# Trading two steps of SyncE's queue at the end of a rotated tile

## The reference

```
h = rmsnorm(x, norm_g[i]);  proj = h @ w_in[i]
A: forgetting attention, 8 heads x 64        (qa, ka, va, fa, za)        no rotary
B: sparse attention, 8 query heads, 2 groups (qb, kcb, vcb, ksb, vsb, kwb, vwb, gb, zb)
   qb, ksb, kwb go through rope(); compressed, selected and window branches, gated
C: differential attention, 4 heads x 2 maps  (qc, kc, vc, zc)            qc, kc go through rope()
merged = g0 * (ya @ w_br_a) + g1 * (yb @ w_br_b) + g2 * (yc @ w_br_c)
x = x + merged @ w_out;  x = x + sigmoid(x @ w_ple_gate) * (p[i] @ w_ple);  rmsnorm at the end
```

## Time and profile before

| what | value |
|---|---|
| median of three runs | 1498.74 us (1497.97 to 1499.55) |
| profiled execution, its own time | 1496.63 us |
| its span, first to last instruction | 1494.8 us |
| mean granted TensorE clock | 0.997 |
| TensorE matmul busy | 1469.7 us, 98% |
| TensorE weight load busy | 1227.9 us, 82% |
| VectorE busy | 946.6 us, 63% |
| ScalarE busy | 628.0 us, 42% |
| GpSimd busy | 74.7 us, 5% |
| DMA, mean | 101 GB/s, 38.4% of 16 engines' time |

### The profile page before, as it was taken

One profiled execution on the slowest core, in us unless ns is written; L12 is line 12 of the kernel. 1 busy time (PEld: TensorE's weight loads), 2 busy tenths in 40 slices (PEclk: granted clock), 3 DMA queues, 4 the chain that ended last, 5 costly groups with the idle time before them and its releaser, 6 DMA issues.

```text
span 1494.8 us, 21863 instructions
## 1 busy us (share of the span) xinstructions
PE 1469.7 (98%) x7765; PEld 1227.9 (82%) x7765; DVE 946.6 (63%) x2197; ACT 628.0 (42%) x1499; POOL 74.7 (5%) x79
## 2 busy tenths in 40 slices
PE   8999999999999999999999999999999999999997
PEld 6788888888888888888877887888888888878885
DVE  6866766655556676465677667656555667754544
ACT  6543434434344444243444334344344444434333
POOL 1000000000001000000100000000000000000011
PEclk9999999999999999999999999999999999999998
DMA  6334453234235543432342345422343355433322
GB/s 166 94 86 120 106 121 79 64 84 101 77 77 135 140 114 92 115 104 71 99 111 72 105 113 132 102 64 71 87 97 78 102 128 133 118 106 92 103 75 92
DMA packets 259264, 150.51 MB, mean 101 GB/s; under 512 B 47482, under 2 KB 247764, under 8 KB 259156
## 3 DMA queue, kind: packets, MB, share of 16 engines
q1 hardware_dynamic: 259156, 149.11, 38.4%
HBM read 118.67 MB, written 2.10 MB: 81 GB/s over the span
## 4 chain that ended last, share of the span: by engine, by line
PE 89%; DVE 4%; ACT 2%; issue 2%; DMA 1%; SPq 1%; POOL 0%; ACTq 0%; POOLq 0%; DVEq 0%
PE D L764 23%; PE D L766 22%; PE D L765 22%; PE Ob L955 7%; PE T L933 4%; PE S L921 2%; PE S L920 2%; PE S L910 1%; DVE w_lo L1310 1%; PE Mb L971 1%; PE Mb L845 1%; PE Ob L959 1%; DMA arena<-rcs 1%; ACT w_hi L1081 1%; PE D L777 1%
## 5 line engine op out<-in xcount | busy, mean ns | idle before, releaser
L764 PE MATMUL D<-h_hi,w_hi 128*128 128x512 f32 x1264 | 537.5, 425 | 2.7 <-DVE zs L1459 2.7
L766 PE MATMUL D<-h_lo,w_hi 128*128 128x512 f32 x1264 | 496.0, 392 | 0.0
L765 PE MATMUL D<-h_hi,w_lo 128*128 128x512 f32 x1264 | 494.3, 391 | 0.0
L1310 DVE TENSOR_TENSOR w_lo<-raw,w_hi 128x512 fp32r<-128x512 f32 (+2 forms) x504 | 292.4, 622 | 162.5 <-ACT w_hi L1081 162.2
L1189 ACT ACTIVATE probs<-probs,nmax 128x128 f32<-128x128 f32 (+3 forms) x256 | 142.0, 556 | 399.1 <-DVE nmax L1559 399.1
L1081 ACT ACTIVATE w_hi<-raw 128x512 fp32r<-128x512 f32 (+2 forms) x504 | 256.7, 558 | 60.7 <-DMA raw<-in_w_in_dram 44.9
L766 PEld LDWEIGHTS D<-h_lo,w_hi 128*128 128x128 f32 x1264 | 237.2, 188 | 53.1
L764 PEld LDWEIGHTS D<-h_hi,w_hi 128*128 128x128 f32 x1264 | 238.8, 189 | 43.7 <-issue 4.6
L765 PEld LDWEIGHTS D<-h_hi,w_lo 128*128 128x128 f32 x1264 | 239.4, 189 | 30.4 <-issue 0.5
L1559 DVE CUSTOM_DVE_ANT_0 probs<-S,maskb 128x128 f32<-128x128 f32 (+3 forms) x256 | 115.2, 487 | 40.9 <-PE S L921 25.0
L546 DVE COPY pT<-T 128x128 f32<-128x128 f32 (+3 forms) x160 | 77.7, 488 | 80.4 <-PE T L933 80.0
(11 more groups left out here) (249 smaller groups left out, 1607.0 us busy)
## 6 DMA issues: line engine op xcount, KB each, us to landing
raw<-in_w_in_dram SPq DMA_DIRECT2D x124, 512.0 KB, 4.0
arena<-rcs SPq DMA_DIRECT2D x48, 256.0 KB, 4.4
raw<-in_w_in_dram SPq DMA_DIRECT2D x32, 256.0 KB, 4.0
arena<-rcs SPq DMA_DIRECT2D x64, 128.0 KB, 2.3
raw<-in_w_out_dram SPq DMA_DIRECT2D x16, 512.0 KB, 3.6
raw<-in_w_ple_gate_dram SPq DMA_DIRECT2D x16, 512.0 KB, 3.6
rcs<-rx SPq DMA_DIRECT2D x80, 64.0 KB, 2.0
raw<-in_cmp_w_k_dram SPq DMA_DIRECT2D x8, 512.0 KB, 3.8
```

Of the source, the lines that this page charges most:

```text
L764: pe.matmul(o, w_hi[:, sl, cs], hi[:, k, :], start=(k == 0), stop=False)
L765: pe.matmul(o, w_lo[:, sl, cs], hi[:, k, :], start=False, stop=False)
L766: ins = pe.matmul(o, w_hi[:, sl, cs], lo[:, k, :], start=False, stop=last)
L1310: TT(w_lo[:, sl, half], raw[:, ring(L, t, RAW), half], f(w_hi[:, sl, half]), ALU.subtract).then_inc(M["dve_lo"], 1)
```

## The change

In SyncE's walk over the items, at the end of a tile, the load of the weights of tile t + 4 now stands ahead of the swap. Before it stood behind. Nothing else is changed, and the order on the four other engines is the same.

```
                     for it in items:
+                        if it[0] == "end" and it[1] + 4 < T0 + RAW:
+                            static_load(it[1] + 4)
                         if it[0] == "end" and tiles[it[1]][0] in ROTATED:
 
                             n = rots.after(it[1])
@@
                                 sp.wait_ge(M["put_s"], put_before[tiles[it[1]][:2]])
                             for a, b in ((0, 32), (32, 0), (64, 96), (96, 64)):
                                 sp.dma_start(rs[a:a + 32, :], src[b:b + 32, :]).then_inc(M["sw_ld"], 16)
-                        if it[0] == "end" and it[1] + 4 < T0 + RAW:
-                            static_load(it[1] + 4)
                         if it[0] == "put":
                             place(M, sp, it[1])
```

## The result

| | before | after |
|---|---|---|
| median of seven runs each | 1497.97 us (1496.23 to 1499.55) | 1501.19 us (1501.06 to 1503.72) |
| ratio, 95% interval | | 1.0024 [1.0015, 1.0033] |
| profiled execution, its own time | 1496.63 us | 1501.74 us |
| its span | 1494.8 us | 1499.9 us |
| mean granted clock | 0.997 | 0.996 |

The kernel became slower by 0.24%: 3.6 us by the ratio, 3.2 us by the two medians. The forecast time, 1499.3 us, is 1.9 us off and the measured time is inside the range, but on the question of the sign I had put 0.87 on "within 0.2%" and 0.09 on "slower". The interval of the ratio lies wholly above 1 and straddles the 0.2% line, so "slower, by about the least that can be told" is the right reading, and a forecast of +0.6 us is too small by 3 us. Most of what follows is about those 3 us.

A forecast was written before the change was run, and what follows sets the result against it. TensorE's own work was taken to bound the kernel (busy 1469.7 of a 1494.8 us span). The terms, 0.6 + 0 + 0 - 0 = +0.6 us, gave 1499.3 us on the median's scale of 1498.74, range 1497.3 to 1502.2 us.

The forecast's parts named there:

- within 0.2%: Outcome that the time changes by less than can be told from no change, 0.2% or 3 us; chance 0.87.
- slower: Outcome that the kernel gets slower by more than 0.2%; chance 0.09.
- The six kc tiles: kc 1 to 3, both layers: load hidden in SyncE's standing time, swap lands 0.2 us later on three S starts; +0.6 us.
- x: Delay of the kc swap's landing because it lies behind a load: taken as 0.2 us, bounds 0 and 1.7.
- The slower rival: kc swap queues behind the load's traffic, 1.7 us late, three to six S starts pay: +5.1 to +10.2 us; chance 0.09.
- The 22 others: Rotated tiles other than those six: swap 0 to 1.7 us later, hidden by air; 0, bound 2 us.
- the chain from the qc put to S: At kc 2, from the qc put's landing to S: no air, each microsecond of later swap is one of TensorE.
- A moved product meets other instructions: GpSimd's multiply shifts who is hit on VectorE, up to 1.1 us each way; no named TensorE wait behind it; 0.
- The gain: Weight loads start up to 2.5 us earlier, but ScalarE's rounding waits on its own order; 0, upper bound 3.3 us.
- The dense waits of 1.4 us: TensorE's two waits just before a dense tile, ended by VectorE, 2.7 us together; the forecast was wrong if they went.
- What would show it: Signs in the changed profile: kc 2 swap within 0.2 us of landing, VectorE waits 6 to 8 us, S under 2.5.

The follow-up runs named there:

- e1: Kernel before with the load ahead of the swap only at the kc tiles: 1497.71 us, ratio 1.0004 to before.
- e3: Kernel before with the load ahead of the swap only at the ksb, kwb and qb tiles: 1497.18 us, ratio 1.0001 to before.
- e2: Kernel before with the load ahead of the swap only at the qc tiles: 1501.30 us, ratio 1.0031 to before.
- the three parts: The change split by tile: load first at kc alone (e1), qc alone (e2), or ksb, kwb and qb alone (e3): 1.0004, 1.0031, 1.0001.
- e7: Changed kernel with the qc tiles' cosT product, add, split and put two k steps earlier: 1498.65 us, ratio 1.0006 to before.
- e8: Kernel before with the qc tiles' cosT product, add, split and put two k steps earlier: 1496.18 us, ratio 0.9992.
- e4: Changed kernel with the pow ahead of the product of qc 2 and qc 3 in GpSimd's queue: 1504.15 us, ratio 1.0050 to before.
- e5: Kernel before with three 32-byte DMAs in front of each qc swap, no load moved: 1498.89 us, ratio 1.0005.
- e6: Kernel before with the load first, but at qc 1 to 3 only one of two brb DMAs ahead of the swap: 1499.23 us, ratio 1.0010.

## Why the prediction was right or wrong

**The time and the range: in part luck.** 1501.19 lies inside the range, but the range was made for another mechanism: its upper part took a kc swap up to 0.9 us late on three starts of S. Its base, 1498.74, was also 0.8 us above the median of seven runs; counted from 1497.97 the same sum and range would have been 1498.6 and 1496.5 to 1501.4, with the measured time just inside.

**The six kc tiles (+0.6): the mechanism right, the cost too small to tell.** The load in the standing time, the swap 0.07 us after the landing, the put behind which a load is issued landing at 2.2 to 2.4 us, the swap at 2.0 to 2.1. From the first issue to the last landing the kc swaps 2 and 3 took 3.96, 4.32, 4.40 and 3.90 us, before 3.90, 4.10, 4.30 and 3.84: x was 0.1 on average, not 0.2. e1 puts the price of the kc tiles at 0.04% [-0.05, 0.13], 0.6 us with bounds of -0.8 and 1.9, which tells 0.6 from 0 no more than from 1.5. The slower rival, that the kc swap queues behind the load, did not happen: no kc swap DMA took over 2.9 us.

**The 22 others (0): this step failed.** I wrote that the swap would be up to 1.7 us later and "the air larger", at most 1.4 for the others (qc 3 was 1.8), having compared the end of GpSimd's product with the add that needs it, at one tile, ksb. For ksb the outcome was right (e3: 1.0001), though not by the sum: the load took SyncE 0.37 us to issue and not 1.34, so the swap was 0.8 us late and not 1.7, and then its DMAs, behind a load of 512 KB, took 3.2 to 4.3 us in place of 2.0 to 2.8. VectorE waited 0.73 us at the add, hidden as I had said. For qc 2 and 3 the same look would have found 3.3 to 4.7 us of air in front of the add, and it would have misled me: the air that counts is between the product and the next thing in GpSimd's queue. In the kernel before, the pow ends only 0.3 to 0.7 us before the Newton step starts. I had looked at SyncE's queue, in which the step moves, and not at the queue of the engine that the moved step feeds. I had even named the chain from the qc put to S as one with no air, and then treated the qc tile, which is its beginning, as one of 22 without consequence. The term put at 0 measured 2.9 us of S starts in the profile and 1.6 of clock on top, of which 0.8 us and, it may be, the clock are owed to one slow DMA; by the ratios the qc tiles carry 0.31% in e2 and 0.24% in the whole change.

**A moved product meets other instructions (0): this failed too.** I had the rule and a row for it and argued that no named wait of TensorE lay behind "these products". I had looked only at what the product with cosT loses. The split of the weights is also an instruction of two SBUF inputs, it is 1.3 us long and comes at the end of each tile, and at qc 0 the moved product now meets it: 1.10 us on VectorE, 0.9 on TensorE. At qc 0 of the second layer it was the very case I had named, the product with cosT losing 0.34 us, and TensorE lost 0.4. The sentence that by the rule "both orders leave one of them waiting" is true and was the wrong comfort, since the two do not have the same slack.

**The gain (0): right.** The dense waits of 1.4 us are unchanged, and none of the three parts is faster.

**What would show it.** The swap's start, the brb load in standing time, busy time within 1 us and the dense waits came as said. The two that failed are VectorE's waits for GpSimd at the add, 9.9 us against 6 to 8, and S, 3.1 us against 2.5. One put DMA in front of a load, at qc 2 of the second layer, took 2.6 us against my limit of 2.5; before it took 2.5.

**The chances.** 0.09 for slower was too little for a change that could make 22 swaps later (18 were, by 0.4 to 1.8 us) when I had looked at one of them.

## What to carry to other kernels

A transfer that is issued 1.4 us later is late for everything behind its consumer in the consumer's queue, not for its reader alone: list what stands next in that engine's order, and measure the air there. If moving one item of a queue turns a wait into a longer instruction, look for missing room and not for a better order. Placing the reader earlier in its own queue took back most of the loss here (e7, 0.24% to 0.06%); what it gives the kernel before (e8) is at the edge of what can be told. And do not read a cause from the waits of one trace when they scatter by a microsecond between kernels of the same median.

## What the runs showed of the hardware

**The clock drops after a gap of 2 us.** After the start-up, TensorE's gaps of 0.9 to 1.51 us (some forty in the twelve traces) were followed by matmuls of at most 0.48 us. The two longer ones, 2.06 and 2.35 us, were each followed, 1.4 and 0.7 us after they ended, by 3.4 us at half the granted clock, with matmuls of 0.63 in place of 0.39 us, and the first cost 1.6 us more on top of the gap. How a gap between 1.51 and 2.06 us would fare none of them shows. In these traces one wait of 2 us was thus dearer than four of 0.5.

**The excluded engine pays the remainder.** Where the product (1.29 us alone) came first, w_lo took 1.10 longer; where one of VectorE's (w_lo or the product with cosT, 0.68 each) came first, GpSimd's product took 1.36 to 1.79. One of the two w_lo instructions of a tile can be hit, or both engines a little: 1.67 and 1.78 at qc 2 of the first layer after the change, against 1.29 and 1.29.

**A transfer behind a load.** It depended on the size of the load. Swap DMAs of 64 KB behind two brb DMAs (128 KB each) took 2.0 to 2.9 us to land at qc 2, qc 3, kc 2 and kc 3, but for one of 3.8; with no load in front they took 1.9 to 2.5, but for four of 3.0 to 3.4. Behind one load of 512 KB (ksb, kwb, qb 0, qb 3) all 32 took 2.7 to 4.3, against 1.9 to 2.1 before (2.4 and 2.8 for two of ksb). So the slow put of the earlier trace rows, 3.5 to 4.0 behind 512 KB, was a fair guide for these and not for the kc tiles. The swap of kwb in the first layer, before and after:

```profile
DMA to landing us min/median/max: 2.0/2.0/2.0
```

```profile
DMA to landing us min/median/max: 2.7/3.1/3.7
```

**A put with a slow DMA.** The DMAs of the qc 2 and qc 3 puts land in 2.2 to 2.6 us in most places, and up to 3.0 in one of e4 and one of e5, but e1, e4 and e6 have one put each with a DMA of 3.6, 4.2 and 3.8. In the first two a load was issued right behind the put, in e6 none was. What makes them slow stays open.
